# Expert blocks with the gate/up product in two halves and weights cast three blocks ahead; final rows written out with gains loaded in the expert stage

## The reference, cut to what matters

```python
def hier_moe(h, lw):
    ...
    combine = jnp.sum(jax.nn.one_hot(expert_ids, N_EXPERTS, dtype=jnp.float32) * weights[..., None], axis=1)
    hidden = (jax.nn.silu(jnp.einsum('nd,edf->nef', hf, lw['w_exp_gate']))
              * jnp.einsum('nd,edf->nef', hf, lw['w_exp_up']))
    y = jnp.einsum('nef,efd->nd', hidden * combine.astype(hf.dtype)[..., None], lw['w_exp_down'])
...
    x = x + gate2 * hier_moe(h, lw)
...
    y_prompt = rms_norm(xp, final_norm_g)
    y_sample = rms_norm(xs, final_norm_g)
```

## Time and profile before

| | us |
|---|---|
| three runs: median (lowest to highest) | 1359.76 (1357.14 to 1360.11) |
| the profiled execution, its own time | 1359.61 |
| its span, first to last instruction | 1357.8 |
| up to the first instruction of the expert stage | 919.95 |
| expert stage | 366.65 |
| final stage | 71.20 |

### The profile page before, as it was taken

How to read it: one execution, slowest core, us unless ns; L and a number is a source line. 1 busy time by engine, 2 the same in 40 slices (tenths; PEclk the granted TensorE clock), 3 DMA queues, 4 the chain that set the end, 5 groups by cost and what they waited for, 6 DMA issues and landing times. The chain is left out here.

```text
span 1357.8 us, 19140 instructions
## 1 busy us (share of the span) xinstructions
PE 1116.0 (82%) x5908; PEld 934.1 (69%) x5908; DVE 799.6 (59%) x1230; ACT 651.5 (48%) x1048; POOL 437.8 (32%) x295
## 2 busy tenths in 40 slices
PE   4899999979885896998995999936999999999600
PEld 1687777759885785988884888835777777777500
DVE  1754543026454585777773567565778667787277
ACT  2641111123232573666665456205868677878322
POOL 0000000030003393466761000003666557576341
PEclk8899999989997897999997999956999999999855
DMA  9418577131001806235003433136876977633274
GB/s 358 166 62 300 193 231 251 55 98 41 16 1 30 203 33 159 53 93 144 32 16 110 142 107 112 47 110 227 287 270 233 351 270 259 225 117 111 86 272 168
DMA packets 127091, 204.90 MB, mean 151 GB/s; under 512 B 19264, under 2 KB 89824, under 8 KB 124974
## 3 DMA queue, kind: packets, MB, share of 16 engines
q1 hardware_dynamic: 118108, 176.90, 39.3%
q0 software_dynamic: 7344, 26.74, 6.1%
q10 hardware_dynamic: 1570, 0.38, 0.2%
HBM read 215.61 MB, written 45.01 MB: 192 GB/s over the span
## 5 line engine op out<-in xcount | busy, mean ns | idle before, releaser
L88 POOL TENSOR_TENSOR moe_wd_lo<-moe_wd,moe_wd_hi 128x1024 fp32r<-128x1024 f32 x66 | 163.5, 2499 | 104.0 <-ACT moe_wd_hi L2121 104.0
L88 DVE TENSOR_TENSOR moe_wgu_lo<-moe_wgu,moe_wgu_hi 128x1024 fp32r<-128x1024 f32 x132 | 173.0, 1371 | 39.9 <-ACT moe_wgu_hi L2115 37.0
L2115 ACT CAST moe_wgu_hi<-moe_wgu 128x1024 fp32r x132 | 128.7, 1051 | 65.6 <-DMA moe_wgu<-in_w_exp_up 65.1
L93 PE MATMUL proj_acc_ps<-proj_w_hi,hidden_hT_hi 128*128 128x512 f32 x288 | 117.8, 409 | 6.7 <-DVE hidden_hT_lo L88 6.7
L95 PE MATMUL proj_acc_ps<-proj_w_hi,hidden_hT_lo 128*128 128x512 f32 x288 | 115.0, 399 | 0.0
L94 PE MATMUL proj_acc_ps<-proj_w_lo,hidden_hT_hi 128*128 128x512 f32 x288 | 114.5, 398 | 0.0
L93 PE MATMUL moe_gu_ps<-moe_wgu_hi,moe_xT_hi 128*128 128x512 f32 x264 | 106.2, 402 | 4.7 <-DVE moe_xT_lo L88 4.7
L1278 POOL TENSOR_TENSOR att_e<-att_e 128x1152 f32<-128x1152 f32 (+1 forms) x36 | 86.1, 2391 | 74.1 <-DVE att_e L1345 74.1
L94 PE MATMUL moe_gu_ps<-moe_wgu_lo,moe_xT_hi 128*128 128x512 f32 x264 | 105.7, 400 | 0.0
L95 PE MATMUL moe_gu_ps<-moe_wgu_hi,moe_xT_lo 128*128 128x512 f32 x264 | 105.6, 400 | 0.0
L1296 ACT ACTIVATE att_e<-att_sc_ps,att_shift 128x1152 f32<-128x1152 f32 (+1 forms) x72 | 81.5, 1132 | 39.4 <-DVE att_shift L1334 39.2
(11 more groups left out here) (353 smaller groups left out, 2716.6 us busy)
## 6 DMA issues: line engine op xcount, KB each, us to landing
moe_wgu<-in_w_exp_gate SPq DMA_DIRECT2D x34, 1024.0 KB
moe_wgu<-in_w_exp_up SPq DMA_DIRECT2D x34, 1024.0 KB
moe_wd<-in_w_exp_down SPq DMA_DIRECT2D x34, 1024.0 KB
scratch_y_slots<-moe_y SPq DMA_DIRECT2D x33, 512.0 KB
proj_raw<-in_w_in SPq DMA_DIRECT2D x32, 256.0 KB, 4.8
proj_feat<-in_w_ada SPq DMA_DIRECT2D x4, 2048.0 KB, 8.7
proj_xh<-in_w_ada SPq DMA_DIRECT2D x4, 2048.0 KB, 9.6
scratch_h<-mix_h SPq DMA_DIRECT2D x9, 512.0 KB, 2.9
```

Source lines behind the costliest of these rows:

```text
L88: return eng.tensor_tensor(low, value, high.bitcast(F32), ALU.subtract)
L93: pe.matmul(out, a_high, b_high, start=start, stop=False)
L2115: act.copy(wgu_hi[:, k.buf, j:j + 2], wgu[:, buf, j:j + 2]).then_inc(gu_hi_done, 1)
```

## The change

Two stages are written anew; all before them is the same. In the **expert stage**:

- `gate_up` is two halves of 12 matmuls. PE's order for block t becomes: first half of gate_up(t+1), turn of hid(t), `turn_x(t+2)`, second half of gate_up(t+1), down product of t.
- `x_high` and `x_low` work in halves of 512 columns with a semaphore each; the first half waits only for the first half product (`gu_half_done`).
- ACT's order: both halves of `x_high(t+2)`, `silu(t+1)`, first two pieces of `gu_high(t+3)`, y copy of t, last two pieces of `gu_high(t+3)`, `d_high(t+2)`.
- DVE's order: hidT of t, last piece of `gu_low(t+2)`, `x_low(t+2)`, `hidden(t+1)`, first three pieces of `gu_low(t+3)`.
- POOL's order: `gather(t+4)`, low down weights of t+2. There are still two `xg` buffers, so gather(k) waits for `turn_x(k-2)`.
- SP's order is the same; in the block before the last, three DMAs load the final stage's gate rows and gain into the raw gate/up buffer 0.

In the **final stage** the loops are written out; index columns are not copied (the gather reads `slot_of` itself); there are four gather buffers and three out buffers; the mean of squares is kept for every tile, and reciprocal and refinement are done for two tiles at once (tiles 0 and 1, 2 and 3, 4 and 5, 6 and 7, then 8). DVE's order is residuals 0, 1, 2, norm of 0 and 1, residuals 3, 4, norm of 2 and 3, and so on.

The core of the diff:

```diff
@@ expert stage, SP
+                if left == 1:
+                    sp.wait_ge(gu_lo_done, BLOCKS + 2)
+                    load_final_gains(sp, I, W, M)
@@ POOL
             def body(t, left):
+                if left >= 4:
+                    gather(t.next().next().next().next())
                 if left >= 2:
-                    gather(t.next().next())
-                buf = weight_buffer(pool, t)
-                pool.wait_ge(d_hi_done, t.n + 1)
+                    d_low(t.next().next())
...
             gather(Step(0, 0))
             gather(Step(0, 1))
+            d_low(Step(0, 0))
+            gather(Step(0, 2))
+            gather(Step(0, 3))
+            d_low(Step(0, 1))
@@ PE
+            def gate_up(k, half):
+                pe.wait_ge(x_lo_done[half], k.n + 2)
+                if half == 0:
+                    pe.wait_ge(gu_lo_done, k.n + 3)
+                    pe.wait_ge(hid_done, k.n + 1)
+                for j in range(half * (KT // 2), (half + 1) * (KT // 2)):
...
+            def body(t, left):
+                if left >= 1:
+                    gate_up(t.next(), 0)
+                turn_hidden(t)
                 if left >= 2:
                     turn_x(t.next().next())
+                if left >= 1:
+                    gate_up(t.next(), 1)
                 pe.wait_ge(hidT_done, t.n + 2)
@@ ACT
             def body(t, left):
                 if left >= 2:
-                    gu_high(t.next().next())
-                if not (isinstance(t.n, int) and t.n == 0):
-                    evacuate(Step(t.i, t.c - 1))
+                    x_high(t.next().next(), 0)
+                    x_high(t.next().next(), 1)
                 if left >= 1:
-                    d_high(t.next())
                     silu(t.next())
+                if left >= 3:
+                    ahead = t.next().next().next()
+                    buf = weight_buffer(act, ahead)
+                    gu_high(ahead, buf, range(0, KT // 2, 2))
+                evacuate(t)
+                if left >= 3:
+                    gu_high(ahead, buf, range(KT // 2, KT, 2))
                 if left >= 2:
-                    x_high(t.next().next())
...
+                    d_high(t.next().next())
+
+            gu_high(Step(0, 0), weight_buffer(act, Step(0, 0)), range(0, KT, 2))
             d_high(Step(0, 0))
+            x_high(Step(0, 0), 0)
+            x_high(Step(0, 0), 1)
@@ DVE
             def body(t, left):
-                hidden(t)
-                if left >= 2:
-                    gu_low(t.next().next())
                 dve.wait_ge(h_turned, t.n + 3)
                 dve.wait_ge(y_done, t.n + 2)
                 dve.tensor_copy(hidT_hi[:], h_ps[:, 0:FF])
                 dve.drain()
                 split_low(dve, hidT_lo[:], h_ps[:, 0:FF], hidT_hi[:]).then_inc(hidT_done, 1)
                 if left >= 2:
+                    gu_low(t.next().next(), range(KT - 2, KT, 2))
                     x_low(t.next().next())
+                if left >= 1:
+                    hidden(t.next())
+                if left >= 3:
+                    gu_low(t.next().next().next(), range(0, KT - 2, 2))
@@ final stage, POOL
+            for t in range(TILES):
+                if t >= NB:
+                    pool.wait_ge(x3_done, t - NB + 1)
                 for c, dst in enumerate((ya, yb)):
...
+                                            bass.IndirectOffsetOnAxis(ap=slot_of[:, t, c:c + 1], axis=0)).then_inc(y_in[t % NB], 16)
@@ DVE
+            dve.wait_ge(W["final_in"], 16 * 3)
...
+            def normalise(first, n):
+                r = rstd[:, first:first + n]
+                dve.wait_ge(sq_done, first + n)
                 dve.reciprocal(r, r)
-                refine(dve, r, ssq[:, t.buf:t.buf + 1], 1.0 / D, tmp[:])
...
+            for t in range(TILES):
+                residual(t)
+                if t >= 2 and t % 2 == 0:
+                    normalise(t - 2, 2)
+            normalise(TILES - 1, 1)
```

More of the change, by code:

```diff
@@ L2108, in _, with gu_high @@
             act.sem_inc(y_out, 16)
[L2110 to L2114 removed]
+            def gu_high(k, buf, pieces):
+                if pieces[0] == 0:
+                    act.wait_ge(gu_in[k.buf], k.nth * 32 + 32)
+                    act.wait_ge(gu_done, k.n + 1)
+                for j in pieces:
                     act.copy(wgu_hi[:, k.buf, j:j + 2], wgu[:, buf, j:j + 2]).then_inc(gu_hi_done, 1)
@@ L2197, in _, with final_gains, load_final_gains @@
             x_low(Step(0, 1))
+            hidden(Step(0, 0))
+            gu_low(Step(0, 2), range(0, KT - 2, 2))
             blocks(dve, body)
+def final_gains(W):
+    rows = W["wgu"][:, 0].rearrange("p k n -> p (k n)")
+    return [rows[:, c * D:(c + 1) * D] for c in range(3)]
+def load_final_gains(sp, I, W, M):
+    gate0, gate1, gain = final_gains(W)
+    for cond, gate in enumerate((gate0, gate1)):
+        sp.dma_start(gate, row_bcast(M["mods"][cond, GATE2 * D:(GATE2 + 1) * D])).then_inc(W["final_in"], 16)
+    sp.dma_start(gain, row_bcast(I["final_norm_g"])).then_inc(W["final_in"], 16)
@@ L2214, in final_stage @@
         block = ctx.enter_context(nc.Block())
-        started = s.sem("started")
         x2, slot_of = W["x2"], W["slot_of"]
-        def tiles(eng, body, first=lambda t: None):
-            first(Step(0, 0, NB))
-            body(Step(0, 0, NB), True)
-            loops = (TILES - 2) // NB
-            with eng.Fori(0, loops) as i:
-                for c in range(1, NB + 1):
-                    body(Step(i, c, NB), True)
-            for n in range(loops * NB + 1, TILES):
-                body(Step(0, n, NB), n < TILES - 1)
@@ L2229, in is_first @@
[L2229 to L2230 removed]
+        *gate, gain = final_gains(W)
         @block.sync
         def _(sp):
[L2234 to L2244 removed]
+            for t in range(TILES):
+                sp.wait_ge(out_done, t + 1)
+                rows = I["y_prompt"][0] if t == 0 else I["y_sample"][0, (t - 1) * P:t * P, :]
+                sp.dma_start(rows, out[:, t % NO]).then_inc(out_stored[t % NO], 16)
+            for u in range(NO):
+                sp.wait_ge(out_stored[u], 16 * (TILES // NO))
@@ L2264, in body @@
+            for t in range(TILES):
+                act.wait_ge(x3_done, t + 1)
+                act.activation(junk[:], x2[:, t], ACT.Square, scale=D ** -0.5, accum_out=ms[:, t:t + 1])
                 act.drain()
-                act.activation(rstd[:, t.buf:t.buf + 1], ssq[:, t.buf:t.buf + 1], ACT.Sqrt, bias=epsc[:, 0:1],
-                               scale=1.0 / D).then_inc(sq_done, 1)
-            tiles(act, body)
+                act.activation(rstd[:, t:t + 1], ms[:, t:t + 1], ACT.Sqrt, bias=epsc[:, 0:1]).then_inc(sq_done, 1)
@@ L2296, in _ @@
-            tiles(dve, body, residual)
+                dve.tensor_tensor(x2[:, t], x2[:, t], ya[:, u], ALU.add).then_inc(x3_done, 1)
+            def normalise(first, n):
+                r = rstd[:, first:first + n]
+                dve.wait_ge(sq_done, first + n)
+                dve.reciprocal(r, r)
+                refine(dve, r, ms[:, first:first + n], 1.0, tmp[:, 0:n])
+                for t in range(first, first + n):
+                    if t >= NO:
+                        dve.wait_ge(out_stored[t % NO], 16 * (t // NO))
+                    dve.scalar_tensor_tensor(out=out[:, t % NO], in0=x2[:, t], scalar=rstd[:, t:t + 1], in1=gain, op0=ALU.mult,
+                                             op1=ALU.mult).then_inc(out_done, 1)
```

149 lines of the change are left out of this document (58 added, 91 removed).

## The result

The changed kernel takes **1343.25 us** (median of four runs, 1338.99 to 1349.58) against 1359.43 for the kernel before in the same session: ratio 0.9883, interval 0.986 to 0.991. That is 1.2% faster, 14 us short of the forecast of 1329.

What follows compares the result with a forecast made beforehand. Experts were taken as bound by PE, weight loads through SP and, where clustered, DMA bandwidth; the final stage by DVE. Gains of 21.0 and 10.1 took 1359.61 to 1328.5, plus 0.5 for hand-overs: 1329 us, range 1321 to 1342.

Steps and rivals of the forecast that it cites:

- (d): DVE per expert block: 7.3 us of work plus 1 us of meeting POOL, at most 2; 8.3 to 9.3, under 9.6.
- (b): ACT per expert block: 8.7 us against 9.6, including 0.7 for a register load, so ACT is not the bound.
- first rival: Split engines DVE and POOL, or ACT, hold blocks at 9.9 us; sign: gu splits of 6.6 everywhere; 1335; chance 0.18.
- (c): Weight-load loop through SP: y copy 1.9 us earlier, so two loaded blocks take 19.4 instead of 21.30.
- Covered by 1.7: SP's next gate/up load: DVE's last low piece ends at 8.7 us, SP arrives at 10.4, so no wait.
- second rival: Weight loads stay late, the loop through SP keeps 21.3 us, about 11 us of gain lost; 1340; chance 0.15.
- (a): PE in expert blocks: cutting gate_up in two removes 0.4 us of waiting; 9.5, taken as 9.6 per block.
- (e): PE's turn of hidden: needed 5.6 us after gate_up instead of 8.4; chain of about 2.6, covered by 3.0.
- (f): Experts' gathers on POOL: asked for earlier, still two buffers; POOL busy 7.0 of 9.6 us; costed at nothing.
- (g): Start of the expert stage: PE's pause and low clock avoided; net 2.5 us at block 2, 2.0 kept at block 5.
- (h): End of the expert stage: PE's 1.02 us stand for hidT goes, with 0.1 of refill; gain 1.1.
- Final rows: Final stage: DVE starts at 6.8 us (gain 3.8), its chain takes 50.3 (gain 6.7), tail costs 0.4; together 10.1.

Runs made afterwards that it cites:

- kernel 3: Changed kernel with POOL's low down-weight split made for the first two blocks only, so work is left out; 1323.70 us, ratio 0.9737.
- kernel 16: Changed kernel plus SP's and DVE's register loads ahead and first half product waiting for two pieces; POOL still makes both split halves; 1345.47 us.
- Kernel 15: Changed kernel plus half of the down split on DVE, first half product waiting for two pieces, SP's register loads ahead; DVE's register load unmoved; 1341.66 us.
- kernel 9: Changed kernel with the second of a block's two down subtractions made by DVE instead of POOL; 1334.38 us, ratio 0.9808.
- kernel 6: Changed kernel with first half product waiting for two low pieces only and the x split's first half ahead of DVE's last piece; 1341.93 us.
- kernel 1: Changed kernel's expert stage with the old final stage and without the early gain loads; 1351.95 us, ratio 0.9939.
- kernel 10: Changed kernel with SP's six register loads of a block made ahead of its wait for y; 1348.60 us, ratio 0.9890.
- kernel 13: Changed kernel plus half of the down split on DVE, first half product waiting for two pieces, DVE's register load ahead; SP's loads unmoved; 1328.38 us.
- kernel 11: Changed kernel plus half of the down split on DVE, SP's and DVE's register loads ahead, first half product waiting for two pieces; 1325.05 us.
- kernel 14: Changed kernel plus half of the down split on DVE and SP's and DVE's register loads ahead; first half product waits for all pieces; 1322.07 us.
- kernel 12: Changed kernel plus half of the down split on DVE and SP's register loads ahead of its wait for y; 1341.88 us, ratio 0.9850.
- kernel 8: Changed kernel with DVE's register load for the last gate/up piece moved ahead of the wait for hidT; 1341.69 us, ratio 0.9864.

## Why the prediction was wrong, step by step

**The step that failed is (d).** It had DVE at 7.3 us per block and "1 us of meeting, 2 us as the upper bound: 8.3 to 9.3, just under 9.6". The 7.3 was right: 7.16 in kernel 3. The meeting was not: the pieces' mean went to 1.722 us, (1.722 - 1.22) x 4 = 2.0 per block, twice what the sum took and the bound itself, and in the worst block 4.2 on one piece (5.42 less 1.22). (d) had POOL's split beside the x split, hidden and the first piece; in 19 of the 33 blocks it also met the last piece, on which x_low, PE and SP's gate load hang. Second, a term is missing from the sum: DVE's register load between hidT and the last piece, 18.7 us in 31 blocks, 0.6 each. I counted the one on ACT in (b) and not this one. With both, 7.16 + 2.0 + 0.6 = 9.8 us, over PE's 9.5. The experiments show that the meeting is the cause: without it (kernel 3) the plan is met with the register load still in place, and kernel 16 has the meeting without the load and is as slow as the changed kernel. They don't show the same of the load. Kernel 15, with the load and half of the meeting, is as slow too, but kernel 9, which also has both, is 7 us faster. By what path the meeting costs its 20 us, DVE's sum, the few long stops of PE or the late gate loads, isn't separated: kernel 6 took the long stops away and nothing was gained.

Why did mislead? POOL's train beside those four pieces, in the kernel before, is this one:

```profile
1140.87 4.80 POOL L88 TENSOR_TENSOR moe_wd_lo<-moe_wd,moe_wd_hi 128x1024 fp32r<-128x1024 f32 x2 [5.14 <-ACT moe_wd_hi L2121]
```

It ends at 1145.67; DVE's pieces begin at 1143.52 and lose 6.64 - 4.63 = 2.0, close to the 2.15 that the train still runs. I read the 2.0 as the price of a meeting in a block, and it was the price of one meeting with the second subtraction. The change makes more of them, 47 held pieces against 12, often two in a block, and in four blocks the last piece, begun 0.4 to 1.2 us behind the train's start, sat out both subtractions.

**The first rival was right in kind and too small.** "The split engines hold the pace" was priced at 9.9 us a block, 1335. Its sign, splits of 6.6 us in every block, came on average (4 x 1.722 = 6.9). In the loaded blocks 16 to 25 the profiled execution has 11.1, kernel 1's has 10.0. Part of the delay comes in lumps of up to 3.6 us on PE, with the low clock behind each, and I take it that the other blocks' slack can't pay these back; and the last piece is also what SP's gate load waits for, so a held piece sends the next weights late.

**(c) was right as far as it goes.** The pair of loaded blocks was to come from 21.3 to 19.4; in kernel 3 PE turns the hid of blocks 16 and 25 86.36 apart, 19.2 a pair. "Covered by 1.7" for SP's wait on the last piece was wrong: between 1100 and 1240 SP stands 25.4 us in eight stretches for it. The second rival, late loads, is refused by kernel 3, which waits longer for weights than the changed kernel and is 20 us faster; kernel 10 doesn't bear on it. Only when DVE was relieved did SP's loads ahead give some 4 us (13 against 11).

**What held.** (a) 9.5 to 9.6 per block: 9.52 without loads. (b) ACT was not the bound; its halves of x take 0.59 each, 0.55 forecast. (e) PE's waits for hid are 0.5 us in all. (f) no stop for a gather behind the first. (g) by 962 us PE has made 141 matmuls instead of 131, 10 x 0.233 = 2.3 us, with the clock at 1.00 instead of 0.92; 2.5 forecast. (h) one stop of 1.0 us for hidT at the end instead of two. Final rows: first sum 7.1 us into the stage (6.8), 50.6 to the last out (50.3), stage shorter by 9.6 (10.1). With DVE relieved the plan is met: kernel 13 takes 1328.4 against the 1328.5 of the sum. Kernels 14 and 11 pass it, 1322 and 1325, with SP's loads ahead, which the plan didn't have, and in kernel 14 the clustered blocks 11 to 16 gave 6.4 us and not 2.5. That agreement is partly luck: kernel 13 has more work on DVE and less on POOL than the kernel that was summed.

**Not settled:** why SP's loads ahead cost 6 us by the ratio in kernel 12 while they help in kernel 11. Against kernel 9, DVE's register loads are longer there (25.1 us in 30 against 18.4 in 31), 11 pieces are over 3 us instead of 5, and SP waits 110.3 us instead of 31.4 for the last piece, but nothing tells cause from effect. For the same reason it is open what DVE's register load costs by itself; half of the split on DVE with the load ahead and nothing else was not run. That the low clock adds a given amount per stop was read, not tested.

## What to carry to other kernels

When two engines share a path, don't add their overlap as an average: look for the one instruction that sits alone behind the start of the other's train, and follow what is queued behind it. Look at minimum, median and longest of one form: a held instruction counts as busy. Count register loads, on every engine, in the sum. Cutting the other engine's work in smaller pieces can make both wait more often. And leave one remedy out at a time once a combination works: a remedy that shows nothing alone was worth 18 us beside the others. Such a worth holds for that combination only.

## What the runs showed of the hardware that was not expected

- A DVE subtraction with both inputs in SBUF that starts while POOL subtracts waits and ends 1.1 us behind the end of one of POOL's instructions. In the changed kernel that was the one it met in 43 of 47 cases (up to 3.5 us against 1.22 undisturbed), and both of the pair in four (4.6 to 5.4). The Trainium skill (GPSIMD Engine Reference, Key points) says that POOL contends with DVE instructions of two SBUF inputs. The trace agrees, and shows this size.
- POOL is held in turn. 27 of its 33 pairs of subtractions took 5.5 to 6.7 us in the changed kernel, against 4.71 undisturbed; in the kernel before 4 did.
- Cutting POOL's work in eight shared it worse: in 23 of 33 trains the two engines took turns and the train took 6.5 to 10.1 us instead of 5.6, and eight times a DVE piece still sat out the whole train (5.4 to 7.0 us). DVE's median piece went from 1.22 to 1.64 us.
- A register load on DVE in front of an operation kept it idle 0.6 us on average and up to 1.6, 2.2 in kernel 10. With the load moved ahead (kernel 8) this idle time is gone.
